# Second norm of a hybrid flow step: three of seven additions of squares per token half, and four planes' scaling, on GpSimd

## What is computed

```python
out = (gate_a * (x_a @ w_pa) + gate_b * ((cb * conv_u) @ w_pb)) @ w_o
x = x + gt1 * out
xn = rms_norm(x, norm2_g) * (1.0 + sc2) + sh2
x = x + gt2 * (jnp.square(jax.nn.relu(xn @ w_ff1)) @ w_ff2)

def rms_norm(x, g):
    return x * lax.rsqrt(jnp.mean(x * x, axis=-1, keepdims=True) + EPS) * g
```

## Time and profile before

| | |
|---|---|
| median of 3 runs | 2710.09 us |
| lowest, highest | 2707.01, 2713.76 us |
| profiled execution: its own time | 2705.67 us |
| its span | 2703.6 us |
| TensorE busy | 2580.1 us, 95% |
| VectorE busy | 1852.0 us, 68% |
| ScalarE busy | 1080.2 us, 40% |
| GpSimd busy | 1175.8 us, 43% |
| share of TensorE in the chain that ended last | 85% |
| share of VectorE in it | 7% |

### The profile page before, as it was taken

How to read it: one execution, slowest core, us unless ns; L and a number is a source line. 1 busy time by engine, 2 the same in 40 slices (tenths; PEclk the granted TensorE clock), 3 DMA queues, 4 the chain that set the end, 5 groups by cost and what they waited for, 6 DMA issues and landing times.

```text
span 2703.6 us, 68164 instructions
## 1 busy us (share of the span) xinstructions
PE 2580.1 (95%) x28864; PEld 2430.1 (90%) x28864; DVE 1852.0 (68%) x3010; ACT 1080.2 (40%) x1978; POOL 1175.8 (43%) x1154
## 2 busy tenths in 40 slices
PE   4899999999999998999999997999799999999998
PEld 3899999999999996788878887999799999999998
DVE  3464665846748464787766666799778679678686
ACT  3434243342433422433333343443453353443534
POOL 1323222322223224555555544656446556565662
PEclk8999999999999999999999999999899999999999
DMA  8333425435254363444454456454223232333231
GB/s 323 106 110 109 144 69 181 125 97 158 62 174 128 94 193 108 131 143 144 138 154 137 139 160 195 131 175 105 63 63 79 81 101 70 79 84 102 65 79 71
DMA packets 282412, 329.15 MB, mean 122 GB/s; under 512 B 76288, under 2 KB 215936, under 8 KB 273536
## 3 DMA queue, kind: packets, MB, share of 16 engines
q1 hardware_dynamic: 274448, 278.66, 33.2%
q0 software_dynamic: 5904, 39.32, 6.9%
q10 hardware_dynamic: 1760, 6.82, 0.6%
HBM read 221.83 MB, written 91.36 MB: 116 GB/s over the span
## 4 chain that ended last, share of the span: by engine, by line
PE 85%; DVE 7%; issue 2%; DMA 2%; ACT 2%; SPq 1%; POOL 0%; DVEq 0%; ACTq 0%; POOLq 0%
PE ser L970 18%; PE gbank L970 13%; PE bank L970 11%; PE inv L970 11%; PE gbank L1411 8%; PE inv L1411 8%; PE ser L1411 7%; PE bank L1411 7%; DVE a_sum L2298 1%; DMA ring<-in_wblocks 1%; PE inv L1172 1%; PE bank L1155 1%; DVE a_sum L2302 1%; DVE a_sum L2306 1%; DVE a_lo L2272 1%
## 5 line engine op out<-in xcount | busy, mean ns | idle before, releaser
L952 POOL TENSOR_TENSOR w_lo<-raw_w,w_hi 128x512 fp32r<-128x512 f32 x264 | 425.3, 1624 | 370.2 <-ACT w_hi L1747 370.1
L847 POOL TENSOR_TENSOR wsp<-ring,wsp 128x1024 fp32r<-128x1024 f32 x67 | 210.8, 3146 | 670.7 <-ACT wsp L1513 670.7
L1747 ACT ACTIVATE w_hi<-raw_w 128x512 fp32r<-128x512 f32 x264 | 165.1, 632 | 262.5 <-PE ser L1411 98.4
L970 PE MATMUL ser<-xn_hi,wsp 128*128 128x384 f32 x816 | 217.7, 340 | 6.1 <-POOL xn_lo L853 6.1
L1411 PE MATMUL gbank<-a_hi,w_hi 128*128 128x288 f32 x616 | 185.7, 302 | 30.6 <-POOL w_lo L952 14.6
L970 PE MATMUL gbank<-xn_hi,wsp 128*128 128x384 f32 x800 | 213.0, 339 | 1.1 <-issue 1.1
L970 PE MATMUL bank<-xn_hi,wsp 128*128 128x384 f32 x800 | 211.1, 338 | 2.2 <-POOL wsp L847 2.2
L970 PE MATMUL inv<-xn_hi,wsp 128*128 128x384 f32 x800 | 211.3, 338 | 0.5 <-issue 0.5
L2108 DVE TENSOR_TENSOR gmat<-gbank,gmask 128x1024 f32<-128x1024 f32 x144 | 175.6, 1219 | 49.8 <-PE gbank L970 49.0
L1733 ACT ACTIVATE a_hi<-a_sum 128x1152 fp32r<-128x1152 f32 x88 | 103.1, 1173 | 224.6 <-DVE a_sum L2306 78.0
L970 PE MATMUL gbank<-ub 64*64 64x128 f32 (+1 forms) x3456 | 178.4, 310 | 9.5 <-DVE gmat L2108 5.6
(11 more groups left out here) (398 smaller groups left out, 7534.7 us busy)
## 6 DMA issues: line engine op xcount, KB each, us to landing
ring<-in_wblocks SPq DMA_DIRECT2D x107, 512.0 KB, 4.8
ub<-op_d SPq DMA_DIRECT2D x144, 256.0 KB, 2.8
raw_w<-in_wquads SPq DMA_DIRECT2D x33, 1024.0 KB, 4.8
raw_w<-in_wquads POOLq DMA_DIRECT2D x22, 1024.0 KB, 8.8
op_d<-ar SPq DMA_DIRECT2D x32, 576.0 KB, 5.4
op_d<-bk SPq DMA_DIRECT2D x32, 576.0 KB, 6.2
raw_w<-in_wquads SPq DMA_DIRECT2D x44, 256.0 KB, 3.3
raw_w<-zsum POOLq DMA_DIRECT2D x11, 1024.0 KB, 12.3
```

What stands on the lines that cost most here:

```text
L847: GT(wsp[s % 2][1][:], ring[(N_ADA_RING + s) % RING][:], wsp[s % 2][0][:].bitcast(F32), ALU.subtract).then_inc(S["wsplit_lo"], 1)
L952: GT(w_lo[n % 4][:], src, w_hi[n % 4][:].bitcast(F32), ALU.subtract).then_inc(S["wl_ok"], 1)
L970: return nc.tensor.matmul(out, lhsT, rhs, start=start, stop=stop)
L1747: A(w_hi[s][:], raw_of(op)[:, m, :].rearrange("p (k c) -> p k c", k=KH), ACT.Copy).then_inc(S["wh_ok"], 1)
```

## The change

GpSimd gets two new pieces of program, and DVE and ACT lose or move the same:

- Additions 1 to 3 of half 0 are done by GpSimd behind the last w_lo of product 17; those of half 1 behind the last w_lo of product 21. DVE keeps additions 4 to 7, which wait for the third by acc_ok.
- The scaling of half 0's planes 4 to 7 of the norm's order is done by GpSimd between the first and the second w_lo of product 21, with a semaphore of its own, xp_ok, for which ACT's shifts wait.
- Squares 0 to 3 of half 0 move on ACT from the head of period 17 to that of period 16.
- One semaphore is freed for this: the load of gf counts on pk_in, which is used up by then, instead of gf_in.

```diff
             for q in range(PRODUCTS):
                 u, op = product_of(q)
@@ GpSimd
+            def norm_adds(h):
+                for i in range(1, KH):
+                    pool.wait_ge(S["sq_ok"], KT * h + i + 1)
+                    if i > 1:
+                        pool.wait_ge(S["acc_ok"], 7 * h + i - 1)
+                    GT(acc[h], sq[h][0] if i == 1 else acc[h], sq[h][i], ALU.add).then_inc(S["acc_ok"], 1)
+
+            def norm_scale():
+                pool.wait_ge(S["rs_ok"], 1)
+                for i in range(KH, KT):
+                    m = N2_ORDER[0][i]
+                    GT(r3[:, m, half_t[0]], x2[:, m, half_t[0]], rs[0], ALU.mult).then_inc(S["xp_ok"], 1)
+
                     w_low(KH * q + m)
+                    if (q, m) == (21, 0):
+                        norm_scale()
+                if q == number(2, 5):
+                    norm_adds(0)
+                if q == number(3, 2):
+                    norm_adds(1)
@@ ScalarE
-                act.wait_ge(S["xs_ok"], KT * h + i + 1)
+                if h == 0 and i >= KH:
+                    act.wait_ge(S["xp_ok"], i - KH + 1)
+                else:
+                    act.wait_ge(S["xs_ok"], KH * h + i + 1)
...
-                if q == 17:
+                if q == 16:
                     for i in range(KH):
                         norm_square(0, i)
@@ VectorE
-                if q == 18:
-                    norm_adds(0, range(1, KH))
...
                     if q == 19:
                         norm_reciprocal(0)
-                    else:
-                        norm_scale(0, range(KH, KT))
                     read_out(q, range(KH, 2 * KH))
-                    if q == 20:
-                        norm_adds(1, range(1, KH))
```

More of the change, by code:

```diff
@@ L466, in flow_step @@
             ws_ok wh_ok wl_ok as_ok ah_ok al_ok o_full read_a read_d final_ok h12_ok post_ok
-            sq_ok acc_ok rs_ok xs_ok n2_ok fin_full fin_sq fin_sum fin_std fin_free fin_out gf_in""".split()
+            sq_ok acc_ok rs_ok xp_ok xs_ok n2_ok fin_full fin_sq fin_sum fin_std fin_free fin_out""".split()
         S = {n: ctx.enter_context(nc.semaphore(n)) for n in names}
@@ L794, in _ @@
                 sp.dma_start(r3[:, k, :], xa_d[k]).then_inc(S["a_in"], 16)
-            sp.dma_start(gf[:], gfin).then_inc(S["gf_in"], 16)
+            sp.dma_start(gf[:], gfin).then_inc(S["pk_in"], 16)
             for u in range(len(DENSE) - 1):
@@ L826, in _ @@
                         x_in("21")
-            sp.wait_ge(S["gf_in"], 16)
+            sp.wait_ge(S["pk_in"], 16 * PAIRS + 16)
             for t in range(NC):
@@ L2452, in final_norm @@
                         gf[:, i * 512:(i + 1) * 512], mul, mul).then_inc(S["fin_free"], 1)
-            dve.wait_ge(S["gf_in"], 16)
+            dve.wait_ge(S["pk_in"], 16 * PAIRS + 16)
             q = PRODUCTS - 1
```

## The result

| | before | changed |
|---|---|---|
| median of 14 runs | 2709.3 us (2703.6 to 2716.0) | 2719.18 us (2714.44 to 2724.22) |
| ratio, 95% interval | | 1.0035 [1.0026, 1.0045] |
| profiled execution: time, span | 2705.67, 2703.6 us | 2722.25, 2720.4 us |

The change makes the kernel 0.35% slower, 9.9 us between the medians, where 2718.8 us had been forecast.

What follows compares the result with a forecast made beforehand. TensorE was taken to bound the kernel nearly everywhere, standing idle around the second norm. Terms 3.7 + 2.3 - 2.3 + 5.0 = +8.7 us gave 2714.4 us on the profiled execution, 2718.8 as median; range 2707 to 2724.

Steps and rivals of the forecast that it cites:

- Each addition holds DVE for 1.24 us: First half, end of product 17: three GpSimd additions delay DVE's a_sum and so TensorE's product 18, +3.7 us.
- The clock, +2.3 us: Product 18: the longer idleness of 4.4 us before it lowers TensorE's granted clock, +2.3 us, bounds 0 and 3.5.
- The freed reads, -2.3 us: First half: without the additions, DVE's reads of product 18 keep pace and a_hi begins 2.9 us after its end, -2.3 us.
- The second half, +5.0 us: Second norm sums: GpSimd's sum comes late and its zsum and w_lo slow DVE's last four additions to 1.78 us each.
- a run of six DVE operations: End of product 17: DVE operations with two SBUF inputs, for a_sum and a_lo, running when GpSimd's additions come.
- the 20 us of idleness: TensorE's waits around the second norm, taken as the most that could be won: no more than some 20 us.

Runs made afterwards that it cites:

- e1: Only the change's first half (half 0's additions 1 to 3 on GpSimd, their squares one product ahead), against the kernel before: 2710.61 us, ratio 1.0004.
- e9: Half 0's three additions on GpSimd at product 17's end as in the change, each preceded by a second, unused one: 2707.14 us, single execution.
- e8: Kernel before plus three unused GpSimd memsets of 128x1152 behind the last w_lo of product 17: 2700.56 us, single execution.
- e2: Half 0's three additions on GpSimd, one behind each of the first three w_lo of product 17, against the kernel before: 2707.63 us, ratio 0.9993.
- the second profile: The unaltered changed kernel run once more against the kernel before: 2714.98 us beside 2704.77, ratio 1.0030.
- e5: Changed kernel plus a GpSimd wait for half 1's seventh sum before product 22's zsum and w_lo: 2707.75 us beside 2705.33 for the kernel before, ratio 1.0008.
- e11: Changed kernel with half 0's additions spaced behind product 17's first three w_lo and GpSimd waiting for half 1's seventh sum: 2705.38 us, ratio 1.0003 to the kernel before.
- e7: Kernel before with only the order of work on DVE and ACT altered, GpSimd as before: 2691.09 us beside 2705.33, ratio 0.9948.

## Why the prediction was right, by its steps

- **Each addition holds DVE for 1.24 us, 3.7 in all, and TensorE has no slack.** Product 18 began 4.28 - 0.61 = 3.67 us later. Shown by e1, and by e9, e8 and e2 as to the cause.
- **The clock, +2.3 us.** Right, but not to be relied on to the microsecond: product 18 took 14.5 us and not 13.0 in the first profile, with a mean granted clock of 0.88, so +1.5; in the second profile, in e1 and in e5 it took 15.1 to 15.2, so +2.2. What the forecast left out is the low clock behind the norm sums, which it took as unchanged. Against the profile of before the changed kernel lost 0.9 us less between sums 0 and product 20, 1.1 less between sums 1 and product 22, and 0.6 less in product 23. The two stretches of the changed kernel, product 18 and from sums 0 to product 20 (length, busy time of PE, PEld, DVE, ACT, POOL, granted clock, DMA share, GB/s):

```profile
1905.50:1920.10 14.60, 14.54 (x98) 14.57 (x99) 11.96 (x20) 4.15 (x6) 8.24 (x6) 0.88 0.22 73
1932.10:1944.30 12.20, 11.38 (x73) 11.25 (x74) 3.75 (x11) 1.54 (x3) 1.26 (x1) 0.79 0.10 25
```

- **The freed reads, -2.3 us.** ACT's a_hi of product 20 began at 1922.91, 2.9 us after product 18's end at 1920.04, just as worked out:

```profile
1922.91 2.21 ACT L1754 ACTIVATE a_hi<-r 128x1152 fp32r<-128x1152 f32 x2
```

- **The second half, +5.0 us.** 31.93 - 27.06 = 4.9. The sum ready late, the four additions at 1.75 us (1.78 had been said), the w_lo late by 1.78 us and covered: all three are in the rows. e5 shows that 3.6 of it are collisions; the remaining 1.2 are the wait for GpSimd's third sum.
- **What was luck.** The mechanism and its four terms held, but 2718.8 beside 2719.18 is closer than they can be. The terms measured 3.7, 1.5, -2.3 and 4.9, together 7.8 us, and 8.5 in the second profile; with the losses of clock that were left out, the stretch to product 24 is +5.1 and +5.9 us, where +8.7 had been forecast. The medians say 7 to 12 us and, in the second comparison, 5 to 11. The profile of before had low clock for more of the stretch than e8, which has the same waits (113.5 us against 111.8): measured against e8 the stretch is +6.8 and +7.6, the lower end of the first interval and inside the second. From product 24 to the end of the execution, where nothing is changed, it is 700.3 us before and 700.6 in both profiles of the changed kernel, so nothing of the gap lies there. Why the medians are still 2 to 3 us further apart isn't shown; executions of one kernel spread over more than that.
- **A slip in the forecast.** It speaks of a run of six DVE operations with both inputs in SBUF and lists seven. Nothing hangs on the number, as there are more of them than additions.
- **What the forecast missed.** Of the 20 us of idleness it asked only what DVE's load does to them. e11 shows that six additions and four scalings less on DVE win nothing measurable, and e7 that the order alone is worth 14 us.

## What to carry to other kernels

GpSimd's idle time is no free room for work that reads SBUF while DVE runs operations with two SBUF inputs: each operation moved cost DVE almost its whole length here, 1.2 us of 1.40, so place such work beside DVE's reads of PSUM, or hold GpSimd's own deferrable work back with a wait until DVE's chain is through. And before work goes to another engine, ask of every wait in the chain whether what stands ahead of it in its engine's queue is needed yet: here the norm sums stood behind low halves, scalings and shifts that were needed only later, and another order won 14 us where moving the load won none.

## What the runs showed of the hardware

- GpSimd pays in the collision too: an addition of 576 columns takes 1.40 to 1.43 us alone and 2.54 us beside DVE's 1152-wide operations, DVE's 2.58 us in place of 1.35. They alternate strictly, operation by operation, over six in a row in e9. The Trainium skill, page "SBUF — State Buffer", section "Who interferes with whom", has a DVE instruction with two SBUF inputs contend with a GpSimd instruction that reads SBUF, and calls the contention "an exclusive lock"; the rows agree, with 1.2 us held for an operation of 1.40.
- GpSimd's memsets of 1152 columns, 1.1 us each, did not hold DVE (e8). The same section of the Trainium skill says that a GpSimd instruction which only writes SBUF does not contend with such a DVE instruction; the row agrees.
- How long an idle stretch is does not alone decide whether the clock falls. After 2.23 us of idleness before product 18 in e2 the product took 12.97 us, with a granted clock of 1.00, all at 2.4 GHz; after 1.78 us in e11 it took 14.49 us, part of it at 1.2 GHz. After 4.3 us it took 14.5 to 15.2, and after 7.88 us, in e9, 14.6. An estimate from these rows: a term for the clock in a forecast of this kernel is uncertain by some 2 us. The product in e2 and in e11 (columns as above):

```profile
1897.90:1910.90 13.00, 12.98 (x98) 13.00 (x99) 11.86 (x20) 4.01 (x5) 8.19 (x6) 1.00 0.23 82
...
1893.40:1908.00 14.60, 14.51 (x98) 14.54 (x99) 12.01 (x20) 4.12 (x5) 8.30 (x6) 0.88 0.20 73
```
